# A two-layer transformer block on one core: the second layer's later modulation summed as rows by VectorE, weights loaded three steps ahead, and the gate's taps in the product's own bank

## The reference, cut to what matters

```python
def ada_mod(cond, w, b):
    m = jax.nn.silu(cond) @ w + b
    return jnp.split(m[..., None, :], N_MOD, axis=-1)     # sh1, sc1, g1, sh2, sc2, g2
...
def conformer_conv(h, w_pw1, b_pw1, w_dw, b_dw, ln_g, ln_b, w_pw2, b_pw2):
    u = h @ w_pw1 + b_pw1
    a, g = jnp.split(u, 2, axis=-1)
    u = a * jax.nn.sigmoid(g)
    u = depthwise_conv(u, w_dw) + b_dw                    # 31 taps
    u = jax.nn.silu(layer_norm(u, ln_g, ln_b))
    return u @ w_pw2 + b_pw2
def conv_ffn(h, w_up, w_dw, b_dw, w_down):
    u = h @ w_up
    gate, val = jnp.split(u, 2, axis=-1)
    gate = depthwise_conv(gate, w_dw) + b_dw              # 3 taps
    return (jax.nn.gelu(gate) * val) @ w_down
```

## Time and profile before

| what | us |
|---|---|
| median of 3 runs | 1799.84 |
| lowest, highest | 1798.01, 1800.12 |
| the profiled execution, its own time | 1799.43 |
| its span, first to last instruction | 1797.6 |

### The profile page before, as it was taken

How to read it: one execution, slowest core, us unless ns; L and a number is a source line. 1 busy time by engine, 2 the same in 40 slices (tenths; PEclk the granted TensorE clock), 3 DMA queues, 4 the chain that set the end, 5 groups by cost and what they waited for, 6 DMA issues and landing times.

```text
span 1797.6 us, 26460 instructions
## 1 busy us (share of the span) xinstructions
PE 1657.2 (92%) x9589; PEld 1306.1 (73%) x9589; DVE 671.7 (37%) x1279; ACT 751.4 (42%) x1141; POOL 789.2 (44%) x436
## 2 busy tenths in 40 slices
PE   5688997999898999999999799999998899999996
PEld 1566563667888988888888578778876688888884
DVE  2474687444555024433300343443341533333002
ACT  2332341646577444444322244444444444444220
POOL 0453323545577954434455523432326244444551
PEclk9799998999899999999999899999998799999998
DMA  8567897656445742323333211121203123232321
GB/s 305 176 210 208 234 258 233 237 210 215 140 143 156 204 130 94 94 94 93 88 96 98 61 36 42 42 71 53 65 24 106 47 94 93 94 93 86 88 84 47
DMA packets 70798, 222.12 MB, mean 124 GB/s; under 512 B 7872, under 2 KB 15552, under 8 KB 70464
## 3 DMA queue, kind: packets, MB, share of 16 engines
q1 hardware_dynamic: 69568, 217.29, 38.8%
q10 hardware_dynamic: 1152, 3.75, 0.5%
HBM read 215.51 MB, written 5.51 MB: 123 GB/s over the span
## 4 chain that ended last, share of the span: by engine, by line
PE 78%; issue 8%; DVE 5%; DMA 3%; ACT 3%; POOL 2%; DVEq 1%; SPq 0%; ACTq 0%; POOLq 0%
PE bank L1437 19%; PE bank L1439 18%; PE bank L1438 18%; PE bank L1644 3%; PE bank L1645 3%; PE bank L1646 3%; PE bank L1722 2%; PE bank L1744 2%; PE bank L1381 2%; DMA w_raw<-in_cv_w_pw 2%; POOL w_lo L566 2%; PE bank L1407 2%; PE bank L1732 2%; DVE bank L1166 1%; PE bank L1573 1%
## 5 line engine op out<-in xcount | busy, mean ns | idle before, releaser
L566 POOL TENSOR_TENSOR w_lo<-w_raw,w_hi 128x1024 fp32r<-128x1024 f32 (+1 forms) x284 | 665.4, 2352 | 854.4 <-ACT w_hi L712 854.3
L712 ACT ACTIVATE w_hi<-w_raw 128x1024 fp32r<-128x1024 f32 (+1 forms) x284 | 293.3, 1041 | 406.0 <-PE bank L1439 264.0
L1437 PE MATMUL bank<-h_hi_lat,w_hi 128*128 128x512 f32 x888 | 356.3, 401 | 10.9 <-DVE u_lat L1190 5.1
L1438 PE MATMUL bank<-h_lo_lat,w_hi 128*128 128x512 f32 x888 | 352.6, 397 | 0.0
L1439 PE MATMUL bank<-h_hi_lat,w_lo 128*128 128x512 f32 x888 | 352.4, 397 | 0.0
L1437 PEld LDWEIGHTS bank<-h_hi_lat,w_hi 128*128 128x128 f32 x888 | 167.9, 189 | 65.6 <-issue 20.9
L1439 PEld LDWEIGHTS bank<-h_hi_lat,w_lo 128*128 128x128 f32 x888 | 167.9, 189 | 40.6
L1438 PEld LDWEIGHTS bank<-h_lo_lat,w_hi 128*128 128x128 f32 x888 | 168.1, 189 | 39.3
L1437 PE MATMUL bank<-h_hi_ctx,w_hi 128*128 128x256 f32 x560 | 164.6, 294 | 26.9 <-POOL w_lo L566 14.4
L1438 PE MATMUL bank<-h_lo_ctx,w_hi 128*128 128x256 f32 x560 | 160.5, 287 | 0.0
L1439 PE MATMUL bank<-h_hi_ctx,w_lo 128*128 128x256 f32 x560 | 160.3, 286 | 0.0
(11 more groups left out here) (186 smaller groups left out, 2677.0 us busy)
## 6 DMA issues: line engine op xcount, KB each, us to landing
w_raw<-in_ffn_w_up SPq DMA_DIRECT2D x132, 512.0 KB, 3.6
ada_raw<-in_mod_w SPq DMA_DIRECT2D x96, 512.0 KB, 5.4
w_raw<-in_cv_w_pw SPq DMA_DIRECT2D x48, 512.0 KB, 6.2
w_raw<-in_ffn_w_down SPq DMA_DIRECT2D x48, 448.0 KB, 3.4
w_raw<-in_ffn_w_down SPq DMA_DIRECT2D x24, 512.0 KB, 3.5
w_raw<-in_na_w_qkv SPq DMA_DIRECT2D x24, 512.0 KB, 6.0
shifted_lat<-u_lat SPq DMA_DIRECT2D x32, 270.0 KB, 7.4
shifted_ctx<-u_ctx SPq DMA_DIRECT2D x32, 142.0 KB, 2.9
```

Source lines behind the costliest of these rows:

```text
L566: pool.tensor_tensor(wlo[s][:, 0:kt * P], raw[s][:, 0:kt * P], whi[s][:, 0:kt * P].bitcast(F32), ALU.subtract).then_inc(w_lo, 1)
L712: act.activation(whi[s][:, 0:kt * P], raw[s][:, 0:kt * P], ACT.Copy).then_inc(w_hi, 1)
L1437: pe.matmul(b, whi[s][:, w], hi[:, a], start=(first and k == 0), stop=False)
L1438: pe.matmul(b, whi[s][:, w], lo[:, a], start=False, stop=False)
```

## The change

It has four parts.

1. **Modulation.** Four chunks stay on PE: layer 0, and shift and scale of layer 1's first norm. The other 4096 numbers of layer 1, needed for the latent half alone, come as 32 row tiles [128 x 1024] of the transposed matrix: DVE multiplies each half by the silu of `c`, which lies along the free axis in PSUM on all partitions, and sums it (64 instructions). They are loaded and summed in `down0l`.
2. **Loads.** In pw1 SP issues the tiles of step n+3 right behind the write of `u`, ahead of the shifted reads. The blocks of a step's third place come behind the shifted reads, and from step 8 on every second step has none there.
3. **End of pw1.** The tail of blocks is gone. The last convolution and its sum are done behind the second tile of `pw2c`. Step 14 has 24 taps on PE in place of 16. The squares and silus of the latent norm stand at other places in ACT's list, DVE makes `diag_w` ahead of the taps, and the low parts of the context norm are spread over two steps.
4. **Up-projection.** The taps are added in the gate product's own bank. Context phases have two `gate_in` and two `gate`. PE waits for `g_rdy` of two pairs ago before it writes a gate bank. ACT's `w_hi` of a value tile comes behind the gelu.

```diff
-    CHUNKS = 2 * MOD // CHUNK_TILES
+    CHUNKS = (MOD + 2 * KD) // CHUNK_TILES
+    ROW_TILES = 2 * MOD - CHUNKS * CHUNK_TILES
+    ROW_RING = 4
...
-    ADA_AT = [(0, 2, 0), (0, 0, 0)] * (KD // 2) + [(2, 0, 2)] * KD
+    ADA_AT = [(0, 2, 0), (0, 0, 0)] * (KD // 2) + [(2, 0, 2), (2, 0, 0)] * (KD // 2)
...
-    ADA_TAIL = [(done, done + 4), (done + 4, done + 8)]
-    done += 8
...
-    for c in [0, 2] * (KD // 2) + [2] * (KD // 2) + [4] * (KD // 2):
+    for c in [0, 0, 0, 2, 0, 2, 0, 2] + [2, 0, 2, 0, 2, 0, 2, 2]:
...
-            return GROUPS if n == STEPS - 1 else PE_GROUPS[side_of(n)]
+            return {STEPS - 1: GROUPS, STEPS - 2: GROUPS - 2}.get(n, PE_GROUPS[side_of(n)])
...
                 sp.dma_start(u_dram[side][s][:, :], U[side][s][:, :]).then_inc(u_out, 16)
-                ada_loads(ada_from[n][2])
+                step_loads(n + 3)
                 sp.wait_ge(u_out, 16 * (n + 1))
...
                     sp.dma_start(dst, src).then_inc(r_in[side][s], 16)
+                ada_loads(ada_from[n][2])
...
+            def row_load(r):
+
+                if r < ROW_RING:
+                    sp.wait_ge(cond_row_s, 2)
+                else:
+                    sp.wait_ge(row_done, r - ROW_RING + 1)
...
+            rows_at = {4 + i: range(i * ROW_TILES // 20, (i + 1) * ROW_TILES // 20) for i in range(20)}
...
                         if j % 2 == 0:
-                            act.wait_ge(gate_cv, it * 2 + (p0 + p + 1))
-                            act.activation(gate_in[:, 1:n + 1], bank[j][:, 0:n], ACT.Copy).then_inc(gate_t0, 1)
-                            act.wait_ge(g_rdy, it * 2 + (p0 + p + 1))
-                            act.activation(TAPPED[:, 0:n], bank[j][:, 0:n], ACT.Identity,
+                            if not fresh:
+                                act.wait_ge(gate_cv, it * 2 + (p0 + p + 2 - bufs))
+                            act.activation(g_in[:, 1:n + 1], tp, ACT.Copy).then_inc(gate_t0, 1)
+                            act.wait_ge(gate_t0, it * 2 + (p0 + p + 1))
+                            act.activation(tp, tp, ACT.Identity,
...
+                for r in range(ROW_TILES):
+                    dve.wait_ge(row_in[r % ROW_RING], 16 * (r // ROW_RING + 1))
+                    for half in range(2):
+                        w = row_raw[r % ROW_RING][:, half * 512:(half + 1) * 512]
+                        c = half * ROW_TILES + r
+                        dve.tensor_tensor_reduce(out=w, in0=w, in1=COND_ROW[half][:, :], scale=1.0, scalar=0.0,
+                                                 op0=ALU.mult, op1=ALU.add, accum_out=row_sums[:, c:c + 1]
+                                                 ).then_inc(row_done if half else row_half, 1)
...
-                            pe.wait_ge(evac, it * 2 + (ph.evac0 + j // 2 - 1))
+                            if isinstance(it, int) and it == 0:
+                                pe.wait_ge(evac, ph.evac0 + j // 2 - 1)
+                            else:
+                                pe.wait_ge(g_rdy, it * 2 + (up_pairs0[name] + j // 2))
...
-            pw2c_after = {0: lambda: stat_sum(ll, "conv_l"), 1: lambda: ada_turn(3), 3: ln_l_squares,
-                          4: lambda: spread_inverse(ll, 1)}
+            pw2c_after = {1: last_convolution, 2: lambda: stat_sum(ll, "conv_l"),
+                          4: ln_l_squares, 5: lambda: spread_inverse(ll, 1)}
```

More of the change, by code:

```diff
@@ L205, in build @@
                 Yh[side] = sb(f"y_{side}", KD * N[side], on=g)
-                SQ[side] = sb(f"squares_{side}", KD * N[side], on=g)
+                with ExitStack() as h:
+                    SQ[side] = sb(f"squares_{side}", KD * N[side], on=h)
+                if side == LAT:
+                    row_raw = [sb(f"mod_rows{i}", D, on=g) for i in range(ROW_RING)]
             sb(f"h_room_{side}", 2 * KD * N[side])
@@ L264, in build @@
         V_TURNED = bank[2]
-        ADA_T = [bank[5]] * 5 + [bank[7]]
-        TAPPED = bank[5]
+        ADA_T = [bank[5]] * 3 + [bank[7]]
+        COND_ROW = [bank[5], bank[7]]
         w_in = [sem(f"w_in{i}") for i in range(RING)]
@@ L312, in build @@
         summed = sem("summed")
+        conv_summed = sem("conv_summed")
         pads = sem("pads")
@@ L389, in build @@
             n_h += KD * (ch.pre is not None or ln)
-        sums = ["conv_c", "conv_l", "pw2c", "pw2l", "down0c", "down0l", "o", "down1"]
+        sums = ["pw2c", "pw2l", "down0c", "down0l", "o", "down1"]
         sum0 = {name: i * (KD + 1) for i, name in enumerate(sums)}
+        sum0["conv_c"], sum0["conv_l"] = 0, KD + 1
         y_of = {"pw2c": Yb[CTX], "pw2l": Yb[LAT], "down0c": Yh[CTX], "down0l": Yh[LAT], "o": Yh[LAT],
@@ L396, in build, with gate_bufs @@
         up_pairs0 = {name: i * KF for i, name in enumerate(ups)}
+        up_bufs = {name: 2 if phases[name].side == CTX else 1 for name in ups}
+        pads_done = {name: 2 * sum(up_bufs[u] for u in ups[:i + 1]) for i, name in enumerate(ups)}
+        def gate_bufs(name, p):
+            n, i = N[phases[name].side], p % up_bufs[name]
+            return gate_in[:, i * (n + 2):(i + 1) * (n + 2)], gate[:, i * n:(i + 1) * n]
         def bank0(name):
@@ L520, in _ @@
                     ada_loads(ada_from[n][half])
                 spread_u(n)
-            for blocks in ADA_TAIL:
-                ada_loads(blocks)
-            seconds = [phases["pw2c"], phases["pw2l"], phases["up0c"]]
+            step_loads(STEPS + 3)
+            seconds = [phases["pw2l"], phases["up0c"]]
             for t in range(2 * KD):
-                nt = t + RING
-                ph = seconds[nt // KD]
-                load(ph, nt % KD // ph.per, nt % ph.per, nt % KD < RING)
+                ph = seconds[t // KD]
+                load(ph, t % KD // ph.per, t % ph.per, t % KD < RING)
@@ L534, in body @@
                         load(ph, it, j, first)
+                        if ph.name == "down0l":
+                            if it == 0 and j == 3:
+                                cond_row_load()
+                            for r in rows_at.get(it * ph.per + j, ()):
+                                row_load(r)
                         if ph.kind == "qkv" and j % 3 == 2:
                             tables(it, j // 3, first)
-                if ph.name != "up0c":
+                begun = 2 if ph.name == "up0c" else 0
+                if not begun:
                     body(0, True)
                 if ph.iters > 2:
-                    with sp.Fori(1, ph.iters) as it:
+                    with sp.Fori(max(begun, 1), ph.iters) as it:
                         body(it, False)
@@ L628, in body @@
                         lo_ahead(ph, it, j, last)
+                        for step in (steps or {}).get((it, j), ()):
+                            step()
                 loop(pool, ph, body)
@@ L866, in body @@
                                            ).then_inc(evac, 1)
[L867 removed]
                         else:
[L869 removed]
+                            if not fresh:
+                                act.wait_ge(prod, it * 2 + (p0 + p + 3 - bufs))
                             act.wait_ge(gate_cv, it * 2 + (p0 + p + 2))
[L871 to L872 removed]
+                            act.activation(g_out, tp, ACT.Gelu_apprx_tanh).then_inc(gelu, 1)
+                        hi_ahead(ph, it, j, last)
                 loop(act, ph, body, cuts, hooks, inside)
@@ L939, in _ @@
                      {1: pairs_of(square_updated, fc, 1), 6: pairs_of(hi_h, fc, 6)})
+            act.wait_ge(cond_row_in, 16)
+            act.wait_ge(g_rdy, 1 + 2 * KF)
+            for half in range(2):
+                act.activation(COND_ROW[half][:, :], row_raw[0][:, half * 512:(half + 1) * 512],
+                               ACT.Silu).then_inc(cond_row_s, 1)
             y_phase("down0l", "up0l")
```

174 lines of the change are left out of this document (100 added, 74 removed).

## The result

The changed kernel takes 1772.21 us in the median of 4 runs (1770.70 to 1774.08), the kernel before 1798.92 (4 runs, 1793.86 to 1800.12). The ratio is 0.9853, with a 95% interval of 0.9828 to 0.9878. It is faster by 1.5%, as forecast in direction, but by 26.7 us between the medians in place of 49, and it lies 0.2 us above the range.

A forecast was written before the change was run, and what follows sets the result against it. PE held 78% of the chain that ended last, so its work and waits counted. Terms 7.5 + 9 + 13 + 8.5 + 11 + 0 = 49 us cut the span from 1797.6 to 1748.6; forecast 1750 us, range 1736 to 1772.

The forecast's parts named there:

- Term 1: Context steps (57 to 150): 7.5 us saved, with ACT's wait for tiles gone; bounds 14 and minus 3.
- my rival of 20%: Context steps and end of pw1: tiles push the shifted reads back, term 1 minus 2, kernel 1763 us; 20% chance.
- Term 2: Latent steps (150 to 298.8): 9 us saved from fewer blocks, smaller gaps and clock; bounds 3 and 12.
- Term 3: End of pw1 to first `pw2l` tile (298.8 to 368.2): 13 us saved by earlier convolution and shorter norm; bounds 5 and 18.
- The rival that the norm is no shorter: End of pw1: latent norm keeps its length, only the earlier convolution pays; 6.5 us less gain, 1757 us; 13% chance.
- Term 4: `pw2l` (368.2 to 425.2): 8.5 us saved, as 10 of 24 blocks remain; bounds 6 and 10.
- Term 5: `up0c` (425.2 to 578): 10 us saved, mainly by own banks, and 1 at the start of `down0c`; bounds 2 and 15.
- the walk: Step through one `up0c` iteration by instruction durations: 13.0 and 14.6 us, from 14.25 and 15.9; the `g_rdy` wait costs nothing.
- my signs of being wrong: Late shifted reads, PE waiting at context convolutions or for `g_rdy`, DVE still at rows behind `down0l`, clock as low as before.
- Term 6: Rows in `down0l`: 0 us, 64 DVE sums of 49 us covered by PE's work; may cost 49.
- The rival that rows become the bound: `down0l`: row sums slowed by POOL decide from 2.6 us each on, 1803 us at 2.65; 4% chance.

The follow-up runs named there:

- experiment 1: Changed kernel with the two tiles behind the shifted reads in the eight context steps alone: 1767.91 us, ratio 0.9805 to the kernel before.
- Experiment 9: Changed kernel with 34 unused matmuls filling PE's wait for shifted reads in every second context step: 1765.30 us, ratio 0.9813 to the kernel before.
- experiment 2: Changed kernel with the modulation blocks of every second context step behind convolution and shifted reads: 1758.57 us, ratio 0.9758 to the kernel before.
- Experiment 7: Changed kernel with the shifted reads ahead of the two tiles in the last step of pw1 alone: 1769.33 us, ratio 0.9826.
- Experiment 5: Changed kernel with ACT's weight copy of a value tile ahead of its gelu in `up0c`, as before the change: 1773.57 us, ratio 0.9845.
- experiment 8: Changed kernel with an unneeded PE wait for the last gelu of the context up-projection ahead of `down0c`: 1772.73 us, ratio 0.9843.
- experiment 10: Changed kernel with DVE summing every half of a row tile twice: 1771.38 us, ratio 0.9848 to the kernel before.

## Why the prediction was wrong

**Term 1 failed, and with it the range.** The step that failed is "The tiles now ahead of them were issued 4 us before them, so I add only 0.5". For an even step that starts at 0 I forecast the reads' issue at 12.1, their landing at 17.2 with that 0.5 in it, and the end of the convolution at 19.9. In the trace, from the step at 105.61: issue at 12.5, last landing at 19.3 (124.94), end at 24.4 (129.98). The issue was right within 0.4. From there to the last landing it took 6.8 us, and 4.65 was forecast without tiles: the term of 0.5 measured 2.2. The last tile landed only at 123.11, behind the first two of the four reads (122.35 and 122.97). In experiment 1, with the tiles behind the reads, the same stretch took 4.6 us (120.00 to 124.56). So the reads were late with the tiles ahead, 4 us of lead or not. The late reads were my rival of 20%, which I priced at a pair of 23.4 us and a kernel of 1763; the pair was 24.3.

The other part I had not counted at all: I wrote the convolution's 2.7 us as a fixed length. What had been, behind the first pair, gaps of 0.3 to 2.8 us became one of 4.1 to 5.4 in each pair, the first included, and each was followed by a convolution that ran for the most part at the low clock, 4.5 to 4.9 us in place of 2.8. The granted clock over two of these convolutions:

```profile
125.00:129.90 4.90, 4.87 (x48) 2.48 (x48) 0.00 (x0) 1.98 (x3) 3.04 (x2) 0.55 1.03 288
149.80:154.20 4.40, 4.40 (x48) 2.59 (x48) 0.00 (x0) 0.00 (x0) 2.34 (x2) 0.61 1.03 305
```

Over the eight steps PE's idle time rose only from 17.1 to 19.2 us; its busy time rose by as much, from 75.1 to 77.3, for the same matmuls. Experiment 9 prices the clock: 7.4 us in four pairs. With it the steps are 4.3 us longer than before, without it they take 89.1 us, 3 less than the 92.2 before. But the kernel before had lost to the clock too, 3.1 us in its own convolutions (22.6 us, against 19.5 in experiment 9), and 92.2 less 3.1 is 89.1 as well. So by this estimate the context steps would have won nothing even with the clock out of both. Experiment 1 prices the order of tiles at about 4 us with its clock, experiment 2 shows that the blocks ahead of the write, which I had taken over as given from before, were the larger lever: 17.6 us.

**Term 2: the right mechanism, a new wait.** The gap ahead of step 15 went as forecast (4.48 us before, 0.42 now). But the chunk's copy, which the change makes one step later, now fell behind the context norm's squares on ACT and cost 5.1 us in one place. I had looked at which blocks leave, and not at where the four copies of a chunk's sums come to stand in ACT's list. With the copy moved the term would be 10.5.

**Term 3: the size right, its parts not.** Counted from the end of step 14's convolution, the last convolution started at 10.3 and ended at 20.2, in place of 8.1 and 15.4: tiles ahead of the reads again, and a granted clock of 0.71 over its 9.9 us. Experiment 7, with the reads ahead, has 8.4 and 17.2, at a clock of 0.81. The norm made up for it: from the end of centring to scaling it was 9.4 in place of 14.4, as forecast (4.5, measured 5.0); from scaling to the last low part 16.8 in place of 20.2 (forecast 2, measured 3.5); and its first steps came 1.3 sooner. That the sum came out within 0.6 us is luck: the convolution gave 1.8 in place of 6.6, the norm what the convolution did not. The rival that the norm is no shorter fell.

**Term 4** was right, 8.3 for 8.5: PE's own work in a stage without gaps.

**Term 5: half.** The iterations with low parts came to 12.7 us (forecast 13.0). Those with the residual came to 15.1 and 15.2 (forecast 14.6): the weight copy behind the gelu lets POOL make its low parts later, beside DVE's additions, and stretches them by 0.8. Experiment 5 shows the 0.8 go when the copy goes back. I had these additions in the walk at their old length. In the changed kernel POOL ran 0.78 us longer beside the additions than in experiment 5, and they took 0.80 longer. It is the first of the two that did: it took 2.12 us in one and 1.32 in the other, and in both ended about 0.55 behind POOL's low part (482.90 against 482.36, and 482.12 against 481.57); the second, with nothing of POOL's beside it, took 0.68 in both. The first iteration was 1.6 us longer, with 3.4 us at 0.50 of full clock (409.3 to 412.7) behind a gap of 2.7 us, where before a gap of 2.5 was followed by none (1.00 from 425.2 to 440.3). And `down0c`, where I expected 1 us at the start, lost 2.2 to the slower pace of experiment 8. Against the forecast the new wait for `g_rdy` was not free, and PE waiting for it was one of my signs of being wrong. PE's waits for it in `up0c` (total, times, longest):

```profile
PE bank L1513 <- DVE g_lo_ctx L1355: 11.1, 5, 4.0
```

These are all of PE's waits there but the first. The tile's `w_lo`, the only other thing that PE waited for, was ready 0.9 us earlier each time (as at 539.82 against 540.72, PE starting at 540.86). I had the two as ending in the other order. So some 6.5 of the 11.1 us would have been waits for `w_lo` in any case, as in the kernel before. What the rest cost the phase no run shows: by these rows an estimate is at most 0.9 us behind each of the two waits, at 476.09 and 540.86, after which PE worked on without a gap of note, and less at the others, where ACT and DVE set the pace.

**Term 6** was right: 685 and 83 ns for a sum forecast at 687 and 80 from another operation, the first 9.4 us into `down0l`, the last done 28 us ahead of the phase's last matmul. The rival that rows become the bound fell, and experiment 10 shows how far off it was.

What stays open: why the context steps take 93.4 to 98.4 us in seven kernels with the same instructions there, what `g_rdy` costs, and what decides at which pace PE comes back from a wait.

## What to carry to other kernels

Behind a write that must be read back, nothing large should be in the queue: here the 1 MB of two tiles, issued some 4 us ahead of the reads, made it 6.8 us from the reads' issue to the last landing in place of 4.6. Count the bytes issued ahead of write and reads, by the pace of their landing and not by how long ago they were issued, and put behind them whatever the next step can still wait for. Do not add up gaps only: where short waits became one long wait in each pair of steps, PE's idle time rose by 2.1 us and, with the clock at 0.87 in place of 0.93, its busy time for the same matmuls by 2.2. When work leaves an engine's list, look at where its helpers (here a copy on ACT) come to stand in the other lists: it cost 5.1 us here.

## What the runs showed of the hardware that was not expected

PE had two paces at full granted clock for the same stream of 256-column matmuls, 113 and 118 ns from start to start. In these traces a pace, once taken behind a wait, was kept until the next wait or until matmuls of another kind came between: in `down0c` for all 528 matmuls, 59.9 or 62.2 us. None of the unbroken stretches of 40 and more such matmuls in the 13 traces holds both: each has a mean of 113.3 to 114.0 ns or of 117.7 to 118.2. The kernel before came into `down0c` by a wait of 1.68 us and had the fast pace; the changed kernel and eight versions of it that came in with no wait had the slow one, which is that of their last restart in `up0c`; experiment 8 put 1.2 us of idle time there and had the fast one, and so had experiment 5, which kept the pace of its last restart. Up-projection and down-projection together took 209.2 us with the useless wait, against 210.3 to 211.0 in the changed kernel and in those with the same code in both, so it more than paid for itself, too little to be seen in the whole time. A wait does not always give the fast pace: some restarts in `up0c` had the slow one, as in the changed kernel behind a wait of 1.46 us at 528.15 (117.7 ns), where one of 2.03 at 460.88 gave 113.5.
